# Two-block model on one core: the first mixer's input columns in another order, its gate, low-rank, scan and key-norm work placed between the product's evictions, and the key norm on one sum per head

## The reference, cut to what matters

```python
z = x @ ev_w_in[j]
y_a = rwkv7_mix(z[..., :A_COLS], ...)      # 3360 columns: r 1024, k 1024, v 1024, w_lo 64, a_lo 64, g_lo 160
y_b = rglru_mix(z[..., A_COLS:], ...)      # 2048 columns: xb 1024, gate 1024
y = jnp.concatenate([y_a, y_b], axis=-1) @ ev_w_out[j]

def rwkv7_mix(z, ...):
    z = z + (token_shift(z) - z) * mu
    r, k, v, w_lo, a_lo, g_lo = split_cols(z, A_SIZES)
    w = -jax.nn.softplus(-(w0 + jnp.tanh(w_lo) @ w2)) - 0.5
    decay = jnp.exp(-jnp.exp(w))
    a = jax.nn.sigmoid(a0 + a_lo @ a2)
    g = jax.nn.sigmoid(g_lo) @ g2
    kk = heads(k * k_k)                                        # 16 heads of 64
    kk = kk / jnp.maximum(jnp.sqrt(jnp.sum(kk * kk, -1, keepdims=True)), 1e-12)
    k = k * (1.0 + (a - 1.0) * k_a)
    # per head a 64x64 state is scanned over the tokens with decay, kk, kk * a, v, k and r
    bonus = (jnp.sum(r * k * r_k, -1, keepdims=True) * v)
    return (group_norm(y) + bonus) * g

def rglru_mix(z, ...):
    xb, gate = jnp.split(z, 2, axis=-1)
    xc = causal_dwconv(xb, conv_w, conv_b)                     # width 4
    r, i = sigmoid(blocks(xc) @ w_r + b_r), sigmoid(blocks(xc) @ w_i + b_i)
    log_a = -B_C * r * softplus(-lam)
    a, u = exp(log_a), sqrt(-expm1(2 * log_a)) * (i * xc)
    h = scan(h = a * h + u)
    return gelu(gate) * h
```

## Time and profile before

| what | value |
|---|---|
| median of 3 runs | 3747.91 us (3745.61 to 3750.14) |
| the profiled execution's own time, and its span | 3747.7 us, 3745.9 us |
| TensorE busy | 3504.6 us, 94% of the span |
| VectorE busy | 2219.0 us, 59% |
| ScalarE busy | 1703.8 us, 45% |
| DMA | 562 MB, mean 150 GB/s |
| chain that ended last | PE 85%, DVE 8%, ACT 4%, issue 3% |

### The profile page before, as it was taken

One profiled execution on the slowest core, in us unless ns is written; L12 is line 12 of the kernel. 1 busy time (PEld: TensorE's weight loads), 2 busy tenths in 40 slices (PEclk: granted clock), 3 DMA queues, 4 the chain that ended last, 5 costly groups with the idle time before them and its releaser, 6 DMA issues.

```text
span 3745.9 us, 56805 instructions
## 1 busy us (share of the span) xinstructions
PE 3504.6 (94%) x23212; PEld 3202.4 (85%) x23212; DVE 2219.0 (59%) x2674; ACT 1703.8 (45%) x2035; POOL 0.2 (0%) x4
## 2 busy tenths in 40 slices
PE   8995988899998998988989999989989999899988
PEld 7884978788888998977888888889979888898878
DVE  5576665566666445544556666654456668556674
ACT  4554222455566333322335565553344455344553
POOL 0000000000000000000000000000000000000000
PEclk9997989999999999999999999999999999999999
DMA  6540014354553444432234555434534433444332
GB/s 256 192 146 1 1 46 157 116 197 180 189 192 144 171 170 148 180 143 82 93 132 180 182 195 183 180 139 181 198 126 170 181 135 135 158 159 180 135 138 110
DMA packets 44790, 562.01 MB, mean 150 GB/s; under 512 B 4801, under 2 KB 6993, under 8 KB 7889
## 3 DMA queue, kind: packets, MB, share of 16 engines
q1 hardware_dynamic: 44624, 559.61, 40.8%
HBM read 557.47 MB, written 2.12 MB: 149 GB/s over the span
## 4 chain that ended last, share of the span: by engine, by line
PE 85%; DVE 8%; ACT 4%; issue 3%; DMA 0%; DVEq 0%; ACTq 0%; SPq 0%
PE bank L678 29%; PE bank L682 15%; PE bank L628 5%; PE bank L624 5%; PE bank L619 5%; PE bank L719 4%; PE bank L722 4%; PE bank L727 4%; PE bank L754 4%; PE bank L738 2%; DVE ring L1790 1%; DVE scr L1790 1%; ACT spl_r L1306 1%; PE bank L773 1%; DVE scr L1796 1%
## 5 line engine op out<-in xcount | busy, mean ns | idle before, releaser
L1790 DVE TENSOR_TENSOR spl_r<-ring,spl_r 128x2048 fp32r<-128x2048 f32 x416 | 952.5, 2291 | 654.1 <-ACT spl_r L1306 652.8
L678 PE MATMUL bank<-all_r,spl_r 128*128 128x512 f32 x5024 | 1214.5, 394 | 4.3 <-ACT spl_r L1306 4.3
L1306 ACT ACTIVATE spl_r<-ring 128x2048 fp32r<-128x2048 f32 x416 | 796.3, 1915 | 714.5 <-PE bank L682 389.9
L678 PEld LDWEIGHTS bank<-all_r,spl_r 128*128 128x128 f32 x5024 | 926.8, 188 | 193.4 <-issue 5.3
L682 PEld LDWEIGHTS bank<-all_r,spl_r 128*128 128x128 f32 x5120 | 656.1, 191 | 24.5
L682 PE MATMUL bank<-all_r,spl_r 128*128 128x256 f32 x5120 | 664.0, 283 | 0.0
L1790 DVE TENSOR_TENSOR dsp_r<-ring,dsp_r 128x1408 fp32r<-128x1408 f32 x128 | 207.4, 1625 | 288.8 <-ACT dsp_r L1306 288.8
L1306 ACT ACTIVATE dsp_r<-ring 128x1408 fp32r<-128x1408 f32 x128 | 176.0, 1380 | 295.5 <-PE bank L727 295.5
L1796 DVE SCALAR_TENSOR_TENSOR scr<-sumbuf,vec,scr 128x255 f32<-128x255 f32 (+2 forms) x379 | 182.1, 483 | 132.2 <-ACT scr L1399 80.7
L619 PE MATMUL bank<-scr_r,spl_r 128*128 128x256 f32 x1536 | 208.7, 289 | 38.4 <-ACT scr_r L1260 36.6
L619 PEld LDWEIGHTS bank<-scr_r,spl_r 128*128 128x128 f32 x1536 | 195.7, 194 | 42.0 <-ACT scr_r L1260 34.0
(11 more groups left out here) (327 smaller groups left out, 3005.6 us busy)
## 6 DMA issues: line engine op xcount, KB each, us to landing
ring<-in_up SPq DMA_DIRECT2D x88, 2048.0 KB, 7.9
ring<-in_down SPq DMA_DIRECT2D x64, 1408.0 KB, 5.9
ring<-in_ib SPq DMA_DIRECT2D x34, 2048.0 KB, 8.3
ring<-in_ev_in SPq DMA_DIRECT2D x22, 2048.0 KB, 7.9
ring<-in_pg SPq DMA_DIRECT2D x16, 2048.0 KB, 8.1
ring<-in_out SPq DMA_DIRECT2D x16, 2048.0 KB, 7.7
ring<-in_in SPq DMA_DIRECT2D x12, 2048.0 KB, 8.1
ring<-in_ev_out SPq DMA_DIRECT2D x8, 2048.0 KB, 8.2
```

Of the source, the lines that this page charges most:

```text
L678: mm(b[:, :], WHI[half][:, kk, :], pair(name, kk), start=kk == 0, stop=False, skip_group_check=True)
L1306: A(high[half], w[:, :, half * P:(half + 1) * P], ACT.Copy).then_inc(S["w_hi"], 1)
L1790: return V.tensor_tensor(out, a, b, op)
```

## The change

The input columns come in another order. First the 16 tiles of the B branch (xb and gate in turn), then the low-rank inputs, then k, r and v; the tile of zeros is no longer multiplied, so 43 halves are left of 44. The pieces have three names, `ea` (9), `eb` (2) and `ec` (11), so that the small weights (`bd`, `lwa`, `lg`, of 1 MB, 0.5 MB and 1 MB) can be loaded between them. The loop goes by halves p = 0 to 42, written out, and after chosen halves each engine does a part of the elementwise work: `bd` after halves 16 to 19, `lw` and `la` after 20 to 23, the square root and the squares of k at p = 28, the rglru scan at 30, the key norm at 29 to 36, the cumulative decay at 33, the exponentials at 35, 38 and 39, the last products at 41 and 42. The key norm is now one sum per head: job `ks` sums each head's squares on one row by eight matmuls of 32 stationary columns, DVE and ACT work on 128x512 in all, and four jobs `kb` spread the result over the head's rows. `bonus`, `lg` (`output_gate`) and `to_tokens(0)` go behind the first and the second level. `x` is loaded again, since its place is used for scratch.

```diff
-    ("ev_in", 22, 4096), ("bd", 1, 2048), ("lora", 1, 4096), ("ev_out", 8, 4096),
+    ("ea", 9, 4096), ("bd", 1, 2048), ("eb", 2, 4096), ("lwa", 1, 1024), ("ec", 11, 4096), ("lg", 1, 2048),
+    ("ev_out", 8, 4096),
...
+EV_TILES = [24, 25, 26] + list(range(8, 16)) + list(range(0, 8)) + list(range(16, 24))
+EV_HALVES = 16 + len(EV_TILES)
...
-            if name in ("bd", "lora"):
-
-                piece_done.append(("nfin", 8))
...
+    for k in (1, 2):
+        piece_done[PIECE0["lg"] - k] = ("nfin", 8)
...
+            load("lg", 0)
+
+            sp.wait_ge(S["elem"], 1)
+            sp.dma_start(xa[:, :], dram["x"]).then_inc(S["in_x"], 16)
             stream("ev_out", 8)
...
+            for p in range(EV_HALVES):
+                wide_half(*place(p), 0, p == 0, 2 if p == EV_HALVES - 1 else 1)
...
+                if p == 29:
+
+                    pe.wait_ge(S["kk_sq"], 8)
+                    b = open_job(("ks", 0))
+                    for a in range(8):
+                        j = 32 * (a % 4)
+                        one = mm(b[j:j + 32, (a // 4) * T:(a // 4 + 1) * T], m("sel", 32), GG[:, a, :], start=True, stop=True)
                     done(one)
...
+                if p == 33:
+
+                    pe.wait_ge(S["kk_rec"], 1)
+                    for j in range(4):
+                        b = open_job(("kb", j))
...
+            pe.wait_ge(S["z_dve"], 27)
             for k in range(4):
                 b = open_job(("vt", k))
...
-            to_tokens(0)
             for tt in range(2):
...
                     level(tt, lv)
+                    if not tt and lv == 0:
+                        bonus()
+                        output_gate()
+                    if not tt and lv == 1:
+                        to_tokens(0)
...
+            for p in range(EV_HALVES + 1):
+                if p < EV_HALVES:
+                    project(p)
...
+                if p in (21, 22):
+                    act.wait_ge(S["xc_used"], 1)
...
+                if p == 25:
+                    act.wait_ge(S["rg_la"], 1)
+                    A(GAP, RSIG, ACT.Tanh, scale=-1.0).then_inc(S["rg_exp"], 1)
+                if p == 26:
+                    A(XT, RSIG, ACT.Exp).then_inc(S["rg_exp"], 1)
+                    A(GG, RSIG, ACT.Exp, scale=2.0).then_inc(S["rg_exp"], 1)
+                if p == 28:
+                    act.wait_ge(S["rg_a2"], 1)
+                    A(GAP, GAP, ACT.Sqrt).then_inc(S["rg_sqrt"], 1)
+                    act.wait_ge(S["z_dve"], 11)
+                    for i in range(8):
+                        A(GG[:, i, :], ZK[:, i, :], ACT.Square, scale=v("kk", i)).then_inc(S["kk_sq"], 1)
...
+                if p == 27:
+                    ve.wait_ge(S["rg_exp"], 3)
+
+                    link(stt(GAP, GG, 1.0, GAP, ALU.add, ALU.mult))
+                    ts(GAP, GAP, 1.3e-35, None, ALU.max).then_inc(S["rg_a2"], 1)
...
+                if p == 30:
+                    b = job_wait(("ks", 0))
+                    ts(KNB, b[:, :], 1e-24, None, ALU.max).then_inc(job_free(JOB[("ks", 0)]), 1)
+                    ve.wait_ge(job_free(JOB[("ks", 0)]), freed(JOB[("ks", 0)]))
                     ve.engine_nop().then_inc(S["kk_sum"], 1)
...
+                    link(V.tensor_tensor_scan(flat(GAP), flat(XT), flat(GAP), 0.0, ALU.mult, ALU.add))
+                if p == 31:
+                    ve.wait_ge(S["xc_act"], 16)
+                    tt(YT[:, 8:16, :], YT[:, 8:16, :], GAP, ALU.mult).then_inc(S["rg_gate"], 1)
+                if p == 32:
                     ve.wait_ge(S["kk_sqrt"], 1)
...
+                    V.reciprocal(KNB, KNB).then_inc(S["kk_rec"], 1)
...
+                if p == 41:
+                    ve.wait_ge(S["bon"], 1)
+                    ve.wait_ge(S["cum_e"], 3)
+                    link(tt(BM, GG, CUM, ALU.mult))
+                if p == 42:
+                    tt(KM, ZK, CUM, ALU.mult).then_inc(S["elem"], 1)
```

More of the change, by code:

```diff
@@ L116, in mixer_jobs @@
     add("la", 4)
-    add("lg", 4)
+    add("ks")
+    add("kb", 4)
     add("vt", 4)
-    add("bonus", 4)
-    add("kbt0", 4)
     for tt in range(2):
@@ L653, in moments, with wide_half @@
                     done(one)
-            def wide_half(name, k, half, i, first=False):
+            def wide_half(name, k, half, i, first=False, count=1):
                 _, rhi, rlo = RHS[name]
@@ L803, in _ @@
[L803 to L816, removed]
-                    done(one)
@@ L1282, in fresh, with split @@
                       scale=float(D ** -0.5)).then_inc(S["h_sq"], 1)
-            def split(name, k, i, per=1, which=(0, 1)):
+            def split(name, k, i, per=1, which=(0, 1), count=1):
                 g = PIECE0[name] + k
@@ L1487, in _, with project @@
-            for k in range(8):
-                b = job_wait(("bd", k))
+            def project(p):
+                if p + 2 < EV_HALVES:
+                    name, k, half = place(p + 2)
+                    split(name, k, 0, 1, (half,), 2 if p + 2 == EV_HALVES - 1 else 1)
+                name, k, half = place(p)
+                if p < 16 and p % 2:
+                    dst = YT[:, 8 + p // 2, :]
+                else:
+                    dst = SE[:, p % 3, :]
+                    if p >= 19:
+                        act.wait_ge(S["z_dve"], p - 18)
+                    elif p >= 3 and (p - 3) % 2 == 0:
+                        act.wait_ge(S["xc_done"], (p - 3) // 2 + 1)
+                    elif p >= 16:
+                        act.wait_ge(S["xc_done"], 8)
+                lows(name, k, half, 0, dst, 2 if p == EV_HALVES - 1 else 1)
@@ L1580, in _ @@
                         solve(1)
+                if not tt:
+                    output_gate()
                 for lv in range(1, 6):
                     level(tt, lv)
+                    if not tt and lv == 1:
+                        to_tokens(0)
                     if tt and lv == 2:
@@ L2011, in _, with project @@
-            ve.wait_ge(S["cum_e"], 1)
-            halves = lambda ap: ap.rearrange("p a (t n) -> p a t n", t=2)
-            for tt_ in range(2):
-                one = stt(AR[:, :, tt_, 0, :], T1[:, :, tt_ * P:(tt_ + 1) * P], -1.0, T2[:, :, tt_ * P:(tt_ + 1) * P],
-                          ALU.mult, ALU.mult)
-            one.then_inc(S["cum_l"], 1)
+            def project(p):
+                if p + 2 < EV_HALVES:
+                    name, k, half = place(p + 2)
+                    split(name, k, 0, 1, (half,), 2 if p + 2 == EV_HALVES - 1 else 1)
+                name, k, half = place(p)
+                add_low(name, k, half, 0, YT[:, 8 + p // 2, :] if p < 16 and p % 2 else SE[:, p % 3, :])
@@ L2159, in _ @@
                     level(th, lv)
+                    if not th and lv == 0:
+                        bonus()
                     if th and lv == 0:
```

485 lines of the change are left out of this document (268 added, 217 removed).

## The result

| what | before | after |
|---|---|---|
| median, and its runs | 3747.03 us (3745.61 to 3750.14, 4 runs) | 3714.56 us (3712.02 to 3716.7, 4 runs) |
| ratio, with its 95% interval | | 0.9912 (0.9895 to 0.9929) |
| span of the profiled execution | 3745.9 us | 3712.5 us |

The account below looks back on a forecast made before the run. PE bounds the kernel (busy 94% of the span, 85% of the last chain). From 3747.7 us: product +23.0, behind it -72.1, levels +11.1, `ev_out` piece +10.9, sum -27.1, say 3721, range 3701 to 3737.

Parts of the forecast that it names:

- The product: Input product: removed work, added jobs, waits and clock sum to +23.0 us; end moves from 271.5 to 294.5.
- the ring: Halves 20 to 22: `lwa` loads only once `bd` leaves slot 0; PE waits +2.0 us at `la`'s second job.
- The clock: Behind the waits before `ks` and `kb`: the clock drops, costing 2 x 1.8 = +3.6 us.
- what went: Input product: half of zeros -5.56, `kkn` -3.43, wait for the sixteen squares with its slow half -4.5 us.
- the price of `ks` and `kb`: Input product: 8 matmuls each at the full 0.43 us, no gain from narrow stationary columns; full bound 6.9.
- Behind the product: The 80.8 us between product and `pairs` shrink: `pairs` starts 8.7 us after the product, -72.1.
- The levels: `bonus` and `lg` at the second level +9.2 us, `to_tokens` +1.9; together +11.1.
- The piece of ev_out: Levels: the first `ev_out` piece lands late, delaying ACT's split and `solve(2)` eviction: +9.1, clock +1.8, together +10.9 us.
- Rival 2: Levels: the `ev_out` piece is not felt, `solve(2)`'s evictions not being last; -38, 3710 us; chance 0.12.
- Rival 1: Product: ACT and DVE keep up, waits before `ks` and `kb` about 1 us each; -39, 3709 us; chance 0.20.
- Rival 3: Product, halves 20 to 41: DVE's extra work slows each pass; gain gone at 1.2 us each; chance 0.08.
- The table load: ACT's pass 26, before `ks`: taken as 1.28 us without drain; by the skill, wait and total 1.4 higher.

Follow-up runs that it names:

- e8: Changed kernel with two extra DVE multiplications by 1.0 (128x2048) in pass 31; single run 3720.31 us.
- e1: Changed kernel with job `ks` behind half 30 instead of half 29; 3712.61 us, ratio 0.9900 to the kernel before.
- e10: The same kernel as e5, unchanged, for a second profile; single run 3701.34 us.
- e2: Changed kernel with the four jobs `kb` behind half 34 instead of half 33; 3712.30 us, ratio 0.9899 to the kernel before.
- e9: e5 plus matmuls with the full 128x128 matrix: eight ahead of `ks`, two ahead of each `kb` pair; single run 3704.86 us.
- e11: e5 plus eight narrow matmuls of one group ahead of `ks` (32 columns) and of `kb` (32 rows); single run 3702.36 us.
- e12: e5 plus a full matmul ahead of each of the first four narrow ones in `ks`, and eight full ones ahead of `kb`; single run 3698.06 us.
- e5: Changed kernel with the moves of e3 and e4 together; 3702.64 us, ratio 0.9870 to the kernel before.
- e4: Changed kernel with ACT's split of `ev_out`'s first half behind the evictions of `solve(2)` and `solve(3)`; 3705.49 us, ratio 0.9887 to the kernel before.
- e3: Changed kernel with `ks` behind half 30 and `kb` behind half 34; 3708.64 us, ratio 0.9890 to the kernel before.
- e7: Changed kernel with two extra DVE multiplications by 1.0 (128x2048) in pass 25; single run 3715.77 us.

## Why the prediction came out right, point by point

**The product, +23.0 forecast, +21.7 measured** (293.18 for 271.45). The waits are close to the forecast's, and the chain runs as it was written, pass for pass. With E(p) as the end of half p, the exponentials end at E(27) + 2.1 (forecast 2.3), `rg_a2` stands at E(28) + 4.9 (5.2), the squares end at E(29) + 4.5 (4.8), the scan at E(31) + 4.8 (4.5) and the reciprocal at E(33) + 5.1 (5.0). In us of PE: half 16 0.7 for 0.5; the ring 1.2 for 2.0, and on the job that was named (`la`, for the bank that the sigmoids held; ACT stood for `in_ec` meanwhile); before `ks` 4.52 for 4.8; before `kb` 5.14 for 5.0: 11.5 for 12.3. The clock fell at the two places named, but the halves behind took only 4.47 and 4.65 instead of 3.65, 1.8 in all for the 3.6 forecast. A third, behind the wait for the ring, took 4.91 and was not forecast; with it the sum is 3.1, close by luck. What a wait costs in clock was not the same from one execution to the next: 1.8 for each of the two in e8, nothing behind the ring's wait of 1.38 in e1 (3.92, as behind any job), 1.6 behind 1.41 in e10. The jobs are the larger error. `bd` took 7.2 (1.96, and 1.73 three times), `lw` and `la` 4 x 1.92 = 7.7, `ks` 1.94 and `kb` 2.11: 18.9 with the slow clock in it, for 20.6. So 20.0 is accounted for (-13.5 for what went). The remaining 1.7 lie in two places, read from start to start of the halves: the four jobs of `lw` and `la` cost 2.2, 2.1, 2.9 and 1.9, 9.1 for 7.7, the third being cut in two by the wait for the ring and ending at a low clock (1.65 for 1.13); and the product's first half took 8.41 for 8.01.

**The term that was wrong** is the price of `ks` and `kb`: I wrote that 64 stationary columns "took 1.84 against 1.91 for 16 with 128", from a group that the earlier trace rows label as at full clock. It was not. The windows of the kernel before, around that group and around the same line later, and the later group in the timeline:

```profile
372.30:374.10 1.80, 1.80 (x18) 0.55 0.00 0
441.90:442.90 1.00, 1.00 (x18) 1.00 0.00 0
```

```profile
441.81 1.09 PE L885 MATMUL bank<-ring,scr 128*64 128x128 f32 x16
```

At full clock the same 16 took 1.09, which is 0.57 of the 1.91. The first group stood at half clock, and that hid just the gain that I was asking about. At full clock `ks` is 1.07 (e1) and `kb` 1.17 (e2) for 3.4 each. The rule of the Trainium skill (TensorEngine Tiling (Array Packing), Theoretical Speedup and Tiling Modes) that 32 columns give four tiles at once was right against my row; e9 measures 3.4x, and e11 and e12 its condition. The prediction had weighed it for `ks` alone; e2's 1.17 shows the same gain for the 32 rows of `kb`. Of the error of 4.6 (6.9 for 1.07 and 1.17) 1.8 was hidden, since the two jobs themselves ran at half clock (1.94 and 2.11). e9 and e12 show in their turn how little it decides: with 10.8 and 7.5 us more work on PE in e5's places, the waits before `kb` (1.4) and the halves (1.1 and 1.4) were gone and `vt` waited 4.1 for 6.3.

**Behind the product, -72.1 forecast, -73.1 measured.** `vt` 4.10 after the last half (4.1), `pairs` after 7.72 (8.7); `vt` took 2.73 for 3.8, as the clock in the stretch was 0.83. The exponentials' products had all fitted beside the product.

**The levels, +11.1 forecast, +10.2 measured** (483.93 - 300.90 = 183.0; before, 525.05 less 352.26 = 172.8). `lg` took 7.14 for 6.9; the rest of this sum was not taken apart.

**The piece of ev_out, +10.9 forecast.** From `nfin` to the last matmul of `ev_out` it is 148.4 (632.37 - 483.93) for 139.7 (664.77 - 525.05): +8.7. The piece lands in 8.27 (8.4), and PE waits 9.14 at L1020. That this is the 9.1 of the sum is chance, since PE stood 0.73 there before as well: the wait grew by 8.4. The lower clock cost 1.3 of the 1.8: from the end of the wait to DVE's next piece it is 5.4 for 4.1. And 1.0 came back that the sum did not have: behind a wait of 2.7 in both kernels, L899 took 2.53 at a clock of 0.76, where the same four matmuls (L844 in the kernel before) took 3.55 at 0.55. 8.4 + 1.3 - 1.0 = 8.7. PE's window behind the wait in the changed kernel, and two windows of the kernel before that hold the same products:

```profile
495.20:498.50 3.30, 3.30 (x63) 0.50 0.96 412
```

```profile
528.00:530.00 2.00, 2.00 (x65) 0.88 0.97 401
530.00:532.00 2.00, 2.00 (x46) 0.50 1.07 434
```

The clock fell to 0.50 there before the change too, but only near 529.5, so the products ahead of that are the ones that slowed down. Rival 2 (not felt) falls by e4: with the split moved, 7.5 to 10.1 us come back (after to e4; e3 to e5, 367.9 to 357.8 from `pairs` to `up`).

**The rest** is -1.0 for 0. Sum: 21.7 - 73.1 + 10.2 + 8.7 - 1.0 = -33.4. Of the 6.3 by which the forecast was too high, the product gave 1.3, the stretch behind it 1.0, the levels 0.9, `ev_out` 2.2, the rest 1.0.

**The rivals.** Rival 1 (waits of 1 us) does not hold in after; e3 comes near its time, but with the jobs moved. Rival 3 (DVE full) does not hold: the halves run at 5.57 without waits from 34 on. e7 and e8 show where it would have begun: in pass 31 each microsecond more on DVE is one on PE, in pass 25 not.

**The table load** was weighed at 1.4 us more by the Trainium skill's page (ScalarE: Activation LUTs, What ACT_TABLE_LOAD costs). ACT's timeline of after:

```profile
191.28 1.28 ACT L1574 ACT_TABLE_LOAD   x1
192.58 1.92 ACT L1574 ACTIVATE xtra<-scr 128x2048 f32<-128x2048 f32 x1
```

The next instruction starts 1.30 behind the start of the load, and the wait before `ks` came to 4.52, not 6.2. Nor is there a gap ahead of the load: the instruction before it ends at 191.27. The trace does not agree with a drain. (The 0.0 in the earlier trace rows is the idle time ahead of the load and could not settle it; in the timeline of the kernel before, that load starts at 324.11 and the next instruction at 325.41, so the prediction's reading was right all the same.)

What stays open: why the wait for the ring (L844) was 1.2 in after, 1.4 in e10 and absent in e5, and why the clock fell behind it in after and e10 (4.98 and 5.54 for the half) and not in the eleven other traces of versions of the changed kernel (3.92 to 3.96), with waits of up to 1.47.

## What to carry to other kernels

Before a row becomes a price, look at the clock of its own window: a group that ran at half clock hid a gain of nearly two. Count a job inserted in a busy engine's order by what it waits for and by when that is ready, not by its own length: here the two waits of about 5 us each decided more than the factor of 3.4 in the jobs, and moving the jobs a half later kept only 3.6 of 9.7 us, since the lateness travels with the chain. And look where a load's slot moves when pieces are added: an instruction that waits for it ahead of others on its engine cost 9 us, and one moved line took it back.

## What was not expected of the hardware

- Narrow stationary matrices: eight matmuls of 256 with 32 columns, spread over four groups, 1.07 us; the same eight with 128 columns 3.62; eight with 32 columns into one group's place 3.42; a single narrow one between full ones 0.55. Rows behave alike (1.17 spread, 1.12 for a pair between full ones).
- The clock can fall with no idle time in front. In e11 PE was busy for all of 4.10 us with 32-row matmuls of one group; the clock was 0.86 in it and 0.50 behind it, and the half that followed took 5.61 for 3.82. With 128 rows at the same place (e12) the half behind took 3.96, and with 32 columns of one group in `ks` of the same run the clock stayed at 1.00 (3.92 behind). Why it fell is not shown.
